# A gated feed-forward of three matrices: from interleaved strips to Strassen pairs and a separate down part

## The reference, cut to what matters

```python
D_MODEL, SEQ, D_FF = 1024, 1024, 2816

h2 = modulate(rms_norm(x, ffn_norm_w[i]), sh_f, sc_f)
u = depthwise_conv3(h2 @ w_up[i], conv_w[i], conv_b[i])
gate, val = jnp.split(u, 2, axis=-1)
x = x + g_f[:, None, :] * ((jax.nn.silu(gate) * val) @ w_down[i])
...
def depthwise_conv3(u, w, bias):
    up = jnp.pad(u, ((0, 0), (1, 1), (0, 0)))
    return w[0] * up[:, :-2] + w[1] * up[:, 1:-1] + w[2] * up[:, 2:] + bias
...
def ada_params(cond, w, b):
    m = jax.nn.silu(cond) @ w + b
    return jnp.split(m, 3, axis=-1)
...
lam_bar = jnp.exp(lam * step)
b_bar = ((lam_bar - 1.0) / lam)[..., None] * lax.complex(b_re, b_im)
```

## Time and profile before

| | us |
|---|---|
| runs | 2346.67, 2349.67, 2351.74 |
| median | 2349.67 |
| the profiled execution | 2352.03 |
| its span in the profile | 2350.3 |
| mean granted clock of TensorE | 0.978 |

### The profile page before, as it was taken

One profiled execution on the slowest core, in us unless ns is written; L12 is line 12 of the kernel. 1 busy time (PEld: TensorE's weight loads), 2 busy tenths in 40 slices (PEclk: granted clock), 3 DMA queues, 4 the chain that ended last, 5 costly groups with the idle time before them and its releaser, 6 DMA issues. The chain is left out here.

```text
span 2350.3 us, 29168 instructions
## 1 busy us (share of the span) xinstructions
PE 2219.2 (94%) x11500; PEld 1802.2 (77%) x11500; DVE 1529.1 (65%) x2171; ACT 754.4 (32%) x981; POOL 828.5 (35%) x583
## 2 busy tenths in 40 slices
PE   5999998799999999999999999898999899999998
PEld 3887787588777888888888887587887677777876
DVE  5774516798768988767767566634997554874244
ACT  4103412577333221222222233414223332343331
POOL 0222211531245665656656222210100011588720
PEclk9999998899999999999999999899999899999999
DMA  6595512332312333333334323237247532111132
GB/s 261 197 324 160 160 36 109 108 117 81 145 63 73 113 113 116 116 110 122 113 105 126 97 108 108 81 100 189 98 136 251 199 117 93 66 54 54 47 124 81
DMA packets 118673, 286.33 MB, mean 122 GB/s; under 512 B 11846, under 2 KB 57574, under 8 KB 115432
## 3 DMA queue, kind: packets, MB, share of 16 engines
q1 hardware_dynamic: 115540, 279.36, 35.7%
q10 hardware_dynamic: 3000, 5.15, 0.7%
HBM read 233.31 MB, written 67.93 MB: 128 GB/s over the span
## 5 line engine op out<-in xcount | busy, mean ns | idle before, releaser
L3374 POOL TENSOR_TENSOR w_lo<-w_staged,w_hi 128x1024 fp32r<-128x1024 f32 x66 | 161.4, 2446 | 353.6 <-ACT w_hi L3481 353.3
L276 POOL TENSOR_TENSOR w_lo<-w_staged,w_hi 128x1024 fp32r<-128x1024 f32 x26 | 62.8, 2416 | 374.0 <-ACT w_hi L226 373.8
L2137 POOL TENSOR_TENSOR w_lo<-w_staged,w_hi 128x1024 fp32r<-128x1024 f32 x23 | 58.4, 2540 | 272.1 <-ACT w_hi L2124 272.1
L2145 PE MATMUL ps_in<-h_hi,w_hi 128*128 128x512 f32 x400 | 126.6, 397 | 9.3 <-DVE h_lo L1435 5.2
L3481 ACT CAST w_hi<-w_staged 128x1024 fp32r<-128x1024 f32 x66 | 68.8, 1044 | 179.0 <-PE ps_dn L3401 178.4
L2145 PE MATMUL ps_in<-h_lo,w_hi 128*128 128x512 f32 x400 | 124.1, 391 | 0.0
L2145 PE MATMUL ps_in<-h_hi,w_lo 128*128 128x512 f32 x400 | 124.0, 391 | 0.0
L3226 DVE SCALAR_TENSOR_TENSOR ada_acc<-x_ctx,cond,ada_acc 128x512 f32<-128x512 f32 x112 | 119.7, 1100 | 2.0
L3392 PE MATMUL ps_up<-f_hi,w_hi 128*128 128x512 f32 x336 | 105.1, 394 | 5.1 <-POOL w_lo L3374 2.6
L3392 PE MATMUL ps_next<-f_hi,w_hi 128*128 128x512 f32 x336 | 107.2, 400 | 0.0
L3392 PE MATMUL ps_up<-f_lo,w_hi 128*128 128x512 f32 x336 | 104.0, 391 | 0.0
(11 more groups left out here) (675 smaller groups left out, 6022.5 us busy)
## 6 DMA issues: line engine op xcount, KB each, us to landing
w_staged<-in_w_ff SPq DMA_DIRECT2D x66, 512.0 KB, 3.8
x_ctx<-in_w_ada SPq DMA_DIRECT2D x48, 512.0 KB, 5.3
x_in<-in_w_ada SPq DMA_DIRECT2D x16, 1024.0 KB, 8.1
scratch_bias<-scratch_line SPq DMA_DIRECT2D x32, 512.0 KB, 7.5
att_bias<-scratch_bias SPq DMA_DIRECT2D x32, 512.0 KB, 3.3
w_staged<-in_w_in SPq DMA_DIRECT2D x17, 512.0 KB, 5.4
ada_w<-in_w_ada SPq DMA_DIRECT2D x8, 1024.0 KB, 19.2
scratch_x<-x SPq DMA_DIRECT2D x2, 4096.0 KB, 14.7
```

Of the source, the lines that this page charges most:

```text
L276: nc.gpsimd.tensor_tensor(st.lo[i % 2][:, 0:widths[i]], st.staged[i % 2][:, 0:widths[i]], st.hi[i % 2][:, 0:widths[i]].bitcast(F32), ALU.s ...
L2137: nc.gpsimd.tensor_tensor(st.lo[i % 2][:, :], st.staged[i % 2][:, :], st.hi[i % 2][:, :].bitcast(F32), ALU.subtract).then_inc(st.split, 1)
L2145: last = nc.tensor.matmul(ps[i % 2][:, a:a + BANK], u[i % 2][:, k * P:(k + 1) * P], r[:, k, a:a + BANK], start=(k == 0 and part == 0), sto ...
L3374: nc.gpsimd.tensor_tensor(st.lo[i % 2][:, :], st.staged[i % 2][:, :], st.hi[i % 2][:, :].bitcast(F32), ALU.subtract).then_inc(st.split, 1)
```

## The change

**The up part.** The gate and value strips of the first two j stay as they were. For the other 20 j, the pair (gate strip, value strip) and the two halves of K form a 2 x 2 block matrix, the two halves of K and the two halves of the positions another, and their product is made by Strassen's scheme in Winograd's form: 7 products of 4 x 3 = 12 matmuls of 128 x 512 in place of 8. GpSimd forms four sums of weights a pair (add_weights), GpSimd takes four of the seven low parts and VectorE three, VectorE forms five sums of 512 columns from PSUM (second_sum to second_block), ScalarE copies one product (keep). The sums of the input (PairInputs) are put where x lies, so x goes to memory (x2) ahead of them and comes back in two transfers of 2 MB at the end of the up part. Each merged gated strip is stored, 512 KB, to scratch_ff_a.

**The down part** begins when all 44 up strips are done. It runs in 11 chunks of two rows; in a chunk each of the 8 outputs takes 12 matmuls into one PSUM place, so that there are 88 strips of 12 matmuls and 88 additions into x. The two gated strips and the two rows of weights of a chunk are loaded a chunk ahead, four transfers of 512 KB (load_chunk), rounded by ScalarE, with the low parts by VectorE. All 16 batches of StepMatrices are here, behind strips 3, 8, 13 and so on, 5 apart. A batch's taps are now at partitions 0, 32 and 64 and are stored by 24 transfers of 16 x 128, 8 KB, one for each of 8 lags and 3 groups, in one row of issues. ContextNorm and SplitAhead are here too.

**The conditioning.** The four pieces for both vectors stay in the up part (BothAda, 16 loads, four steps a pair); the eight others go into the projection "u" (LateAda): 2 MB loads, 13 steps of VectorE a strip, and a sum on TensorE behind the strip in which a piece ends.

```diff
-        self.store_lags(sp, b, range(0, 3))
-    def store_lags(self, sp, b, lags):
-        groups = slice((b % 2) * MB, (b % 2 + 1) * MB)
-        for j in lags:
-            sp.dma_start(self.g.dram["toeplitz"][b // 2, j * SH:(j + 1) * SH, groups, :],
-                         self.taps[:, :, CT - 1 - j:2 * CT - 1 - j, :].rearrange("p i e h -> p i (e h)")).then_inc(self.taps_stored, 16)
+        for j in range(CT):
+            for i in range(MB):
+                sp.dma_start(self.g.dram["toeplitz"][b // 2, j * SH:(j + 1) * SH, (b % 2) * MB + i, :],
+                             self.taps[self.STEP * i:self.STEP * i + SH, CT - 1 - j:2 * CT - 1 - j, :].rearrange("p e h -> p (e h)")
+                             ).then_inc(self.taps_stored, 16)
...
-class SecondAda:
...
-    PIECES = 12
-    BOTH = 4
...
+class BothAda:
...
+    PIECES = 4
...
+class LateAda:
...
+    PIECES = 8
+    BATCH = 13
+    BEFORE_PUT = {3: (2,), 4: (3, 4), 5: (5,), 6: (6, 7)}
...
+    def vector(self, dve, i):
+        v = self.nc.vector
+        for n in self.steps(i):
+            p, k = divmod(n, KD)
+            if k == 0:
+                dve.wait_ge(self.loaded[p % 2], self.loaded0 + 16 * (p // 2) + 16)
+                if p >= 2:
+                    dve.wait_ge(self.summed, self.summed0 + p - 1)
+            here, acc, by = self.w[p % 2][:, k * BANK:(k + 1) * BANK], self.acc[p % 2], self.cond[:, k, 1:2]
+            if k == 0:
+                v.tensor_scalar(acc, here, by, None, ALU.mult).then_inc(self.weighted, 1)
+            else:
+                dve.wait_ge(self.weighted, self.weighted0 + n)
+                v.scalar_tensor_tensor(acc, here, by, acc, ALU.mult, ALU.add).then_inc(self.weighted, 1)
...
+class UpPairs:
...
+    PLACES = (0, 2, 0, 2, 1, 2, 1)
...
+    N = KF - FIRST
...
+        for q in range(1, self.N):
+            self.pool_order += [(q, m) for m in (0, 3, 4, 5)]
+            self.dve_order += [(q, m) for m in (1, 2, 6)]
...
+        v.tensor_tensor(s3, self.a11, self.a21, ALU.subtract).then_inc(self.summed, 1)
+        pool.wait_ge(self.summed, 4 * q + 1)
+        v.tensor_tensor(self.a21, self.a21, self.a22, ALU.add).then_inc(self.summed, 1)
+        pool.wait_ge(self.summed, 4 * q + 2)
+        v.tensor_tensor(s2, self.a21, self.a11, ALU.subtract).then_inc(self.summed, 1)
+        pool.wait_ge(self.summed, 4 * q + 3)
+        v.tensor_tensor(s4, self.a12, s2, ALU.subtract).then_inc(self.summed, 1)
...
+    def product(self, pe, q, m):
+        place, (high, low) = self.place(q, self.PLACES[m]), self.inputs[m]
+        self.wait_low(pe, q, m)
+        if m == 2:
+            pe.wait_ge(self.copied, q + 1)
+        if m == 3:
+            pe.wait_ge(self.added, 5 * q + 1)
+        if m == 5:
+            pe.wait_ge(self.added, 5 * q + 2)
+        if m == 6:
+            pe.wait_ge(self.added, 5 * q + 3)
+        for k in range(self.KH):
+            for part, (w, r) in enumerate(((self.st.hi, high), (self.st.hi, low), (self.st.lo, high))):
+                last = self.nc.tensor.matmul(place, self.slot(w, q, m)[:, k * P:(k + 1) * P], r[:, k, :],
+                                             start=(m in self.BEGIN and k == 0 and part == 0),
+                                             stop=(k == self.KH - 1 and part == 2),
+                                             skip_group_check=m not in self.BEGIN)
...
+    CHUNKS = KF // 2
+    STRIPS = KD * CHUNKS
+    TURN_AT = [3 + 5 * b for b in range(mats.N)]
...
+            def load_chunk(c):
+                for j in (2 * c, 2 * c + 1):
+                    load_a(j, both_loaded[(j - 2) % 4])
+                    load_w(j)
...
+                if c:
+                    sp.wait_ge(down, KD * c)
+                if 1 <= c < CHUNKS - 1:
+                    load_chunk(c + 1)
...
+                for b in range(mats.N):
+                    if TURN_AT[b] // KD == c:
+                        mats.store_cp(sp, b)
+                        mats.store_rest(sp, b)
...
+            for q in range(N):
+                if q:
+                    for m in (3, 4, 5):
+                        pairs.pool_low(pool, q, m)
+                if q + 1 < N:
+                    pairs.pool_low(pool, q + 1, 0)
+                    sums(q + 1)
...
+            for b in range(mats.N):
+                mats.pool_first(pool, b)
+                mats.pool_second(pool, b)
+                mats.pool_third(pool, b)
...
+            def down_products(j, s):
+                place, (_, w_hi, w_lo), (_, a_hi, a_lo) = places[(KD * (j // 2) + s) % 3], w_parts(j), a_parts(j)
+                for part, (w, r) in enumerate(((w_hi, a_hi), (w_hi, a_lo), (w_lo, a_hi))):
                     for a in range(0, L, BANK):
+                        last = nc.tensor.matmul(place[:, a:a + BANK], w[:, s * P:(s + 1) * P], r[:, a:a + BANK],
+                                                start=(j % 2 == 0 and part == 0), stop=(j % 2 == 1 and part == 2))
                 return last
...
+                if n >= 3:
+                    pe.wait_ge(added, n - 2)
+                if s == 0:
+                    pe.wait_ge(a_low, 2 * c + 2)
+                    pe.wait_ge(w_low, 2 * c)
+                for j in (2 * c, 2 * c + 1):
+                    last = down_products(j, s)
+                last.then_inc(down, 1)
+                if n in TURN_AT:
+                    b = TURN_AT.index(n)
+                    if b:
+                        pe.wait_ge(mats.taken, 2 * b)
+                    mats.turn(pe, b, window)
+                if n - 1 in TURN_AT:
+                    b = TURN_AT.index(n - 1)
+                    pe.wait_ge(mats.bt_out, b + 1)
+                    mats.tap(pe, b, window)
...
+            for n in range(STRIPS - KD):
+                c, s = divmod(n, KD)
+                if n in TURN_AT:
+                    mats.take_turned(act, TURN_AT.index(n), window)
...
+                if s in (2, 4):
+                    split_a(2 * c + 1 + s // 2)
+                    split_w(2 * c + 1 + s // 2)
...
+                    pairs.second_block(dve, q - 1)
+                    taps(j - 1, 1)
+                    taps(j - 1, 0)
+                    pairs.second_sum(dve, q)
+                    merge(j - 1)
+                    pairs.dve_low(dve, q, 6)
+                    ada_steps(q, (0,))
+                    pairs.third_sum(dve, q)
+                ada_steps(q, (1, 2))
+                pairs.last_block(dve, q)
+                if q == N - 1:
+                    low_a(0)
+                ada_steps(q, (3,))
+                if q in ADD_AT:
+                    ada.modulate(dve, ADD_AT[q], pairs.value(j - 1))
+                pairs.third_block(dve, q)
+                if q + 1 < N:
+                    pairs.dve_low(dve, q + 1, 1)
+                    pairs.dve_low(dve, q + 1, 2)
+                else:
+                    low_a(1)
+            pairs.second_block(dve, N - 1)
...
+            for n in range(STRIPS):
+                c, s = divmod(n, KD)
+                add(n)
...
+                if c + 1 < CHUNKS:
+                    if s in (3, 5):
+                        low_a(2 * c + 2 + s // 4)
+                    if s in (4, 6):
+                        low_w(2 * c + 2 + s // 5)
+                if n - 1 in TURN_AT:
+                    mats.take_taps(dve, TURN_AT.index(n - 1), window)
```

926 lines of the change are left out of this document (585 added, 341 removed).

## The result

The changed kernel took **2391.32 us** (median of 4 runs, 2388.47 to 2394.90), the kernel before on the same chip 2350.70 us (4 runs). The ratio is 1.0173, with a 95% interval of 1.0154 to 1.0191: 1.7% slower. The forecast, 2363.3, had the side right and the size wrong, and the measured time lies 1.3 us above its range of 2312 to 2390.

What follows compares the result with a forecast made beforehand. The prediction took the feed-forward to be bound by the columns TensorE streams. Its terms, -54.4 + 5 + 7 + 59 + 7 + 4 - 14 = +13.6, on 2352.0 profiled gave 2365.6, less 2.3 for the median: 2363.3 us, range 2312 to 2390.

Steps and rivals of the forecast that it cites:

- (e): Down part: TensorE runs near half clock after gaps at nine chunk seams; +7 us (0 to 14).
- (d): Down part: 24 tap-store issues a batch on SyncE, 11.4 us, delay loads and cp store at nine seams; +59 us.
- (a): Up part: 20 Strassen pairs take 84 matmuls each where they took 96, 240 fewer; -54.4 us.
- (b): Up part: VectorE's and GpSimd's chained work beside the pairs holds TensorE up; +5 us (0 to 19).
- (g): Feed-forward: of 20 us over the count, 6 stay, the old loop's waits and seams go; -14 us (-20 to -5).
- Rival 2: Up part bound by VectorE and GpSimd, 1.5 us more a pair: +30, 2393 us; chance 0.09 shared with another rival.
- (c): Start of the down part: first batch of matrices ready at 18 us, TensorE wants it at 11; +7 us.
- the chain through the loads: Down part, chunk seams: tap issues, then loads and casts, 21.7 us; VectorE's row late by 0 to 10.8 us.
- the chain through the cp store: Down part, chunk seams: tap issues, loads, cp store, GpSimd's last operations, 31.3 us against TensorE's 26.2; late by 5.
- the first chain: Down part: the chain through the loads, taken to end at VectorE's low parts; 21.7 us.
- (f): Projection "u": TensorE waits 2.2 us for VectorE's first late conditioning piece; with the clock +4 us (1 to 9).
- Rival 1: Down part: SyncE's issues don't bind, 66 us of seams and clock go; 2305 us, break-even 0.40 to 0.41; chance 0.32.

Runs made afterwards that it cites:

- the 3 transfers alone: The changed kernel with a batch's taps stored by 3 transfers in place of 24, the same bytes: 2328.3 us, 0.9904 of the kernel before.
- all three edits of the down part: The changed kernel with 3 tap transfers a batch, chunk loads issued by ScalarE, and transposes after six of GpSimd's operations: 2299.6 us.

## Why the prediction was wrong, step by step

Two terms failed, both by size: (e), the clock, put at 7 and worth 23.6, and (d), SyncE's seams, put at 59 and worth 70.2. A price too high for the taps hid a part of it.

- **(a) The pairs, -54.4 us.** Right: 240 matmuls fewer. A pair took 395.8/20 = 19.8 us, a little over the 19 to 19.5 foreseen. They bring what was forecast, and more than 2% once the rest is out of their way.
- **(b) The up part's helpers, +5.** Right. 1680 matmuls and four pieces of conditioning count 388.4 us, the stretch lasts 395.8, and a part of the 6 us that (g) keeps belongs here. Rival 2 is refuted by 3.1 us of idle time.
- **(c) The first batch, +7.** Right: TensorE waited 6.2 us for it.
- **(d) SyncE, +59.** The mechanism was the one foreseen, seam by seam: 384 issues, 11 to 12.8 us for a batch (11.4 forecast), and nine waits of TensorE where nine were named. The three seams that went to the chain through the loads are the three that I gave to it (behind the last batches of chunks 2, 4 and 7, so that TensorE waited in 3, 5 and 8), and the six others went to the chain through the cp store. What failed is the size: 70.2 us and not 59. The loads' three cost 24.8 where I had 29.1. The cp store's six cost 45.4, 7.6 each, where I had 5: from the start of the row to the transposes it took 33.0 us on the mean and not 31.3, and TensorE needed 25.4 and not 26.2.
- The end of the first chain was another than I had. I let it end at VectorE's low parts, where TensorE lost 1.2 us. It ended at ScalarE's copy of the transposes, which stands behind the wait for the loads in ScalarE's own order. That the sizes still nearly fit is luck. And I took the transposes' wait for all twelve of GpSimd's operations as given; it alone was worth 31 us.
- **(e) The clock, +7: the step that failed most.** It cost about 23.6 us. I had nine gaps with 1.6 us lost behind each and counted half, on the ground that SyncE would set the end there anyway. There were ten gaps, of 5.4 to 9.6 us; behind each TensorE's work took 1.5 to 2.7 us longer than at full clock, 2.1 on the mean, and all of it stands in the 371.6 us beside the waits. A gap of 2.0 us at 1277 cost another 1.6. With the gaps gone the stretch ran at 1.00.
- The rest of the down part. Small waits, 5.4 us in all, were in no term. The work was 266.2 us and not the 271.5 of the prediction's prices: the taps were 16 x 0.83 = 13.3 us cheaper, while the slower first matmuls of strips and the context's few matmuls add 8.0, which the 6 us of (g) cover in part. That saving was luck. Without it the forecast would have been further off.
- The Trainium skill (DMA: Bandwidth & Descriptors, section Issuing engines are not separate DMA queues) says that issuing from several engines saves only the issuing time, usually small beside the transfer. Here the four loads of a chunk moved to a second engine were worth 49 us: they had stood behind 11 to 12.8 us of issues and ahead of the cp store. In the kernel before, the same row of issues was worth nothing, as the page has it.
- The support that I took from the 61.3 us in the earlier trace rows was no support, as the run with the row in the kernel before showed.
- **(f) The projection, +4 beyond the moved records.** 10.3: a wait of 6.2 where I had 2.2, and the clock behind it. I priced a step by the earlier trace rows, 0.75 us, so that the first piece's eight would take 6.0 us; they took 9.9. VectorE's own row of the same operation, 1100 ns on the mean in the earlier trace rows, stood in the next group. A step is 0.75 us where GpSimd is silent, as the run with the low parts by VectorE shows. The Trainium skill (SBUF — State Buffer, section Who interferes with whom) says that VectorE and GpSimd contend only for a port pair that they share, and that this is an exclusive lock. These runs agree: a multiply-add took up to 2.77 us, and a tensor_scalar of 0.48 us took 2.46 beside a GpSimd operation of 2.40.
- **(g) The old loop's seams, -14.** Too careful, with (b): outside the down part the feed-forward gained about 7 us more than the sum had.
- In sum: the down part 27.1 us worse than summed (the clock 16.6, the seams of (d) 11.2, small waits 5.4, (c) 0.8 and the work 5.3 to the good), the rest of the feed-forward 7.4 better, the projection 6.3 worse, 0.7 behind it not foreseen. That is the 26.7 us by which 13.6 fell short of 40.3.
- Rival 1 named the right lever. Its break-even, 0.40 to 0.41 us an issue, was not tested by itself; the time with nothing bound on SyncE was set at 2305; the 3 transfers alone gave 2328.3, and all three edits of the down part 2299.6.
